# A two-block hybrid network on one core: the squares behind a norm are added up by VectorE, and one set of modulation columns is read later

## The reference

```python
mod = silu(c) @ ada_w + ada_b                  # 6 x 1024 columns per hybrid layer
sh_m, sc_m, gt_m, sh_f, sc_f, gt_f = split(mod, 6)
h = rms_norm(x, norm_mix) * (1 + sc_m) + sh_m
x = x + gt_m * (mixers(h @ w_in) @ w_out)      # attention, sparse attention, gated delta rule
h = rms_norm(x, norm_ffn) * (1 + sc_f) + sh_f
gate, up = split(h @ w_gate_up, 2)
x = x + gt_f * ((silu(gate) * up) @ w_down)    # two such layers, then a norm

x = x + attention(rmsnorm(x) @ w_in) @ w_o     # two layers of the second kind
x = x + (conv_gated(rmsnorm(x) @ w_up)) @ w_down
```

## Time and profile before

| | us |
|---|---|
| median of 3 runs (lowest, highest) | 1687.49 (1687.18, 1693.62) |
| the profiled execution, its own time | 1688.19 |
| its span in the profile | 1686.4 |
| PE busy in the span | 1531.1 |
| DVE busy | 1017.7 |
| ACT busy | 811.2 |
| POOL busy | 237.8 |

### The profile page before, as it was taken

How to read it: one execution, slowest core, us unless ns; L and a number is a source line. 1 busy time by engine, 2 the same in 40 slices (tenths; PEclk the granted TensorE clock), 3 DMA queues, 4 the chain that set the end, 5 groups by cost and what they waited for, 6 DMA issues and landing times.

```text
span 1686.4 us, 29656 instructions
## 1 busy us (share of the span) xinstructions
PE 1531.1 (91%) x12458; PEld 1454.6 (86%) x12458; DVE 1017.7 (60%) x1294; ACT 811.2 (48%) x1296; POOL 237.8 (14%) x96
## 2 busy tenths in 40 slices
PE   6989988899989999889999998489999999899997
PEld 3987778899989978789998897378999898799997
DVE  2775457867657645585545433957784545477843
ACT  3754354343347444444434343355664455466642
POOL 0002218534500022350000001210000001000000
PEclk8999999999999999999999898799999999999999
DMA  9435844645544365445347444013543633335442
GB/s 388 173 144 214 291 182 167 249 157 195 193 179 177 117 242 193 150 151 196 141 169 254 164 164 150 1 58 143 199 162 145 219 134 116 134 127 189 168 152 79
DMA packets 30336, 287.85 MB, mean 171 GB/s; under 512 B 2903, under 2 KB 11383, under 8 KB 11800
## 3 DMA queue, kind: packets, MB, share of 16 engines
q1 hardware_dynamic: 29032, 269.51, 43.3%
q0 software_dynamic: 1152, 16.78, 2.6%
q10 hardware_dynamic: 48, 0.05, 0.0%
HBM read 285.23 MB, written 7.39 MB: 174 GB/s over the span
## 4 chain that ended last, share of the span: by engine, by line
PE 77%; DVE 9%; ACT 5%; DMA 3%; issue 3%; POOL 3%; SPq 0%; DVEq 0%; ACTq 0%; POOLq 0%
PE bank L634 22%; PE bank L636 21%; PE bank L635 21%; PE bank L712 2%; DMA ring<-w_out 2%; DVE w_lo L1789 2%; ACT w_hi L1323 1%; PE bank L958 1%; DVE h L2255 1%; PE bank L792 1%; POOL arena L2352 1%; PE bank L736 1%; DMA arena<-ada 1%; POOL arena L2350 1%; PE bank L779 1%
## 5 line engine op out<-in xcount | busy, mean ns | idle before, releaser
L634 PE MATMUL bank<-hi_T,w_hi 128*128 128x256 f32 x2248 | 652.1, 290 | 38.9 <-DVE h_lo L1772 16.4
L636 PE MATMUL bank<-hi_T,w_lo 128*128 128x256 f32 x2248 | 646.5, 288 | 0.0
L1789 DVE TENSOR_TENSOR w_lo<-ring,w_hi 128x2048 fp32r<-128x2048 f32 (+2 forms) x224 | 519.2, 2327 | 199.8 <-ACT w_hi L1323 198.4
L635 PE MATMUL bank<-h_lo,w_hi 128*128 128x256 f32 x2056 | 592.4, 288 | 0.0
L1323 ACT ACTIVATE w_hi<-ring 128x2048 fp32r<-128x2048 f32 (+2 forms) x226 | 392.0, 1735 | 282.6 <-PE bank L636 271.7
L634 PEld LDWEIGHTS bank<-hi_T,w_hi 128*128 128x128 f32 x2248 | 442.4, 197 | 44.3 <-issue 27.8
L636 PEld LDWEIGHTS bank<-hi_T,w_lo 128*128 128x128 f32 x2248 | 441.8, 197 | 0.0
L635 PEld LDWEIGHTS bank<-h_lo,w_hi 128*128 128x128 f32 x2056 | 405.7, 197 | 0.2
L634 PE MATMUL bank<-act_hi,w_hi 128*128 128x256 f32 x704 | 201.1, 286 | 10.6 <-DVE act_lo L1808 8.9
L635 PE MATMUL bank<-act_lo,w_hi 128*128 128x256 f32 x704 | 200.3, 285 | 0.0
L636 PE MATMUL bank<-act_hi,w_lo 128*128 128x256 f32 x704 | 200.3, 285 | 0.0
(11 more groups left out here) (239 smaller groups left out, 1912.2 us busy)
## 6 DMA issues: line engine op xcount, KB each, us to landing
ring<-w_gu SPq DMA_DIRECT2D x22, 2048.0 KB, 7.7
ring<-w_dn SPq DMA_DIRECT2D x32, 1408.0 KB, 6.0
ring<-w_up SPq DMA_DIRECT2D x22, 2048.0 KB, 7.7
ring<-ada SPq DMA_DIRECT2D x16, 2048.0 KB, 8.9
ring<-w_mix SPq DMA_DIRECT2D x11, 2048.0 KB, 7.6
arena<-ada POOLq DMA_DIRECT2D x8, 2048.0 KB, 8.8
ring<-even_in SPq DMA_DIRECT2D x8, 2048.0 KB, 7.7
ring<-odd_in SPq DMA_DIRECT2D x6, 2048.0 KB, 7.7
```

The source lines that it names most:

```text
L634: nc.tensor.matmul(out, wh, xh, start=start, stop=False)
L635: nc.tensor.matmul(out, wh, xl, start=False, stop=False)
L636: return nc.tensor.matmul(out, wl, xh, start=False, stop=stop)
L1789: V.tensor_tensor(w_lo[:, n % SLOTS, at], ring[:, n % SLOTS, at], w_hi[:, u % AHEAD, 0:size].bitcast(F32), ALU.subtract).then_inc(w_lo_rea ...
```

## The change

In the eight norms behind a product, ACT still squares tiles 0 to 5 in pairs, but tiles 6 and 7 one by one. DVE adds the squares: after residual tile 4 it adds squared tiles 2, 3 onto 0, 1; after residual tile 6 it adds 4, 5 onto 0, 1 and then 1 onto 0. PE sums three tiles (0, 6, 7) and not eight. Apart from that, chunk 10 (22) of the modulation is no longer read by PE ahead of `up`: the loop of three turns is split into one turn and two, and the columns are made between them. Norms 0 and 5 stay as they were.

```diff
+    added = [n for n in range(len(norm_input)) if norm_input[n]]
+    sq_before = [sum(5 if norm_input[i] else 4 for i in range(n)) for n in range(len(norm_input))]
...
             def norm_sums(n):
                 for k in range(KT):
-                    if k % 2 == 0:
-                        pe.wait_ge(sq_ready, 4 * n + k // 2 + 1)
+                    if n in added:
+                        if 0 < k < KT - 2:
+                            continue
+                        if k == 0:
+                            pe.wait_ge(sq_added, added.index(n) + 1)
+                        else:
+                            pe.wait_ge(sq_ready, sq_before[n] + k - 2)
+                    elif k % 2 == 0:
+                        pe.wait_ge(sq_ready, sq_before[n] + k // 2 + 1)
                     last = nc.tensor.matmul(bank[:, 7, 0:S], const("ones"), h[:, k, :],
...
                 turns = 11 // SLOTS
                 pe.wait_ge(gemm_freed, t0)
-                with pe.Fori(0, turns) as i:
-                    for j in range(SLOTS):
-                        one(j, i * (2 * SLOTS) + u0 + 2 * j + 1, i * (4 * SLOTS) + t0 + 4 * j - 3)
+                def turn(first, end):
+                    with pe.Fori(first, end) as i:
+                        for j in range(SLOTS):
+                            one(j, i * (2 * SLOTS) + u0 + 2 * j + 1, i * (4 * SLOTS) + t0 + 4 * j - 3)
+
+                if m_next:
+                    turn(0, 1)
+                    modulations(m_next - 1, m_next)
+                    turn(1, turns)
+                else:
+                    turn(0, turns)
...
                 norm_sums(n + 1)
-                pe.wait_ge(std_ready, n + 2)
-                modulations(m + 6, m + 7)
                 up(f"gu{l}", norm_end[n + 1] - KT, m + 7)
...
+                        if j == 3:
+                            for k in (KT - 2, KT - 1):
+                                act.wait_ge(gemm_freed, ph["t0"] + k + 1)
+                                nc.scalar.activation(h[:, k, :], x[:, k, :], ACT.Square).then_inc(sq_ready, 1)
+                            continue
                         act.wait_ge(gemm_freed, ph["t0"] + 2 * j + 2)
...
                     for u in used:
                         if u < ph["u1"] - 1:
                             low(u + AHEAD)
+                    if k in (4, 6):
+                        dve.wait_ge(sq_ready, sq_before[norm_input.index(name)] + k // 2)
+                        ch(V.tensor_tensor(h[:, 0:2, :], h[:, 0:2, :], h[:, k - 2:k, :], ALU.add))
+                    if k == 6:
+                        V.tensor_tensor(h[:, 0, :], h[:, 0, :], h[:, 1, :], ALU.add).then_inc(sq_added, 1)
```

More of the change, by code:

```diff
@@ L331, in hybrid_then_mixture @@
         sq_ready = sem("sq_ready")
+        sq_added = sem("sq_added")
         ssq_ready = sem("ssq_ready")
```

## The result

The changed kernel took 1697.72 us in the median of 10 runs (1692.49 to 1702.81), the kernel before 1687.99 us in the same comparison (10 runs, 1676.16 to 1693.62). The ratio is 1.0054, 95% interval 1.0033 to 1.0076: slower by 9 us, where I had forecast 26. Measured a second time it was 1696.16 us, ratio 1.0088 (1.0057 to 1.0119). The profiled execution took 1692.59 us, its span is 1690.8 us, 4.4 us more than before. It is one of the two fastest of the ten, so the profile shows less than half of the 9.7 us between the medians; what happened in the slower executions, no trace shows.

The account below looks back on a forecast made before the run. The prediction took PE, with 77% of the chain of waits, to bound the kernel: matmuls with holes. Its terms, 1688.2 - 5.9 - 0.1 + 18 + 17 + 1.6 - 5 = 1713.8, gave 1714 us, range 1682 to 1724.

Parts of the forecast that it names:

- The plain norms, -5.9: In dn0, dn1, o0, down0 and down1, the root no longer waits for PE and the last square is shorter: minus 5.9 us.
- o1, -0.1: In the norm after o1, VectorE's sums delay residual tile 7 and take back the gain of 1.2 us: minus 0.1 us.
- The sums in out0 and out1 wait for POOL: Behind out0, VectorE's sums wait for POOL's instructions, so the root starts 8 us late; the same steps behind out1.
- The next product falls into the normalise steps: Behind out0 and out1, POOL's next product begins at 278.6 and 729.9 us, before VectorE's last low part.
- Each remaining step alternates with one POOL instruction: Behind out0 and out1, remaining VectorE steps let in POOL instructions of 6.9, 4.4, 2.2, 1.1 us; terms plus 18, plus 17.
- none hits: Rival: POOL's products miss the normalise steps behind out0 and out1, leaving about 5 us each; 1692 us, chance 0.12.
- The columns moved, +1.6: Four column matmuls between two full tiles of `up` take about 0.8 us of PE, twice: plus 1.6 us.
- The stalls in `up`, -5: In `up`, PE's loads wait 10.2 us for VectorE's gate product; two of four weighings remain, so half goes: minus 5 us.
- Cheap sums: Rival: POOL does not hold the sums behind out0 and out1; 1684 us, chance 0.21, of which 0.09 at or below 1679.
- The table load: Rival: in plain norms the table load moves behind the wait, so they do not shorten; plus 6 us, no chance given.
- The clock behind the longer holes: Rival: PE's clock falls for longer behind holes of 7 us, up to 3 us for each of two norms; no chance given.
- the case that I held most likely: Both POOL products, behind out0 and out1, fall into the normalise steps; 1714 us, own range 1704 to 1724, chance 0.55.

Follow-up runs that it names:

- plain_norms_only: The changed kernel with the old eight-tile sums behind out0 and out1, new sums in the six other norms; 1679.1 us, ratio 0.9930.
- pieces_old_sums: The changed kernel with the old sums in all norms, GpSimd's product in four pieces and its first sum in two; 1673.42 us, ratio 0.9920.
- columns_only: The kernel before with only the columns moved and the loop split, no new sums; 1680.68 us, ratio 0.9929; repeated, 1683.99 us, ratio 0.9984.
- gpsimd_at_root: The changed kernel with GpSimd's product of chunk 10 (22) held until the root of the norm behind out is made; 1689.68 us.

## Why the prediction was wrong

Its own steps, in its own order:

- **The plain norms, -5.9: right, mechanism and size.** The idle time before the root went from 0.93 to 1.07 us to 0.01 us in all five; the roots come 6.1 us earlier in all, the 48th matmuls (behind down1, the root) 5.5 us. That is read between the marks; in the medians a gain of this size did not show (`plain_norms_only`, `pieces_old_sums`).
- **o1, -0.1: right.** The root is 0.07 us earlier, the 48th matmul 0.05 us later.
- **The sums in out0 and out1 wait for POOL: right.** I had put the end of sum 1 0.55 us behind POOL's product, and residual tile 7 at 270.5; it came at 269.4, and POOL had started 0.8 us earlier. In out1 the lengths are the same to 0.01 us.
- **The next product falls into the normalise steps: right.** Forecast 278.6 and 729.9, measured 278.29 and 730.04.
- **"Each remaining step alternates with one POOL instruction": wrong, and this is the step that failed.** It was taken from the waits in the earlier trace rows, in which POOL was already at work when VectorE asked. The reverse stands there once, POOL's product coming 0.36 us into the low part at 250.10 and reading 8.80 us for 7.01, but with no second such instruction right behind that one. Nothing shows POOL coming to a VectorE in full run, and I used the same rule for that. In all four arrivals traced in the changed kernel POOL stayed out, not a step was held, and 18 and 17 us became 6.4 and 7.5. The 21 us between are all but the whole error of the profiled execution (forecast +25.6 against +4.4 in the span). In the medians the error is 16 us; their executions are some 5 us slower than the profiled one, and no trace shows why. Had I bounded the step from both sides, as I should have, the lower end (the row of steps undisturbed, the first low part 5.4 us late; measured 275.96 for 270.21, 5.75) was already worked out in the text. Even the rival "none hits" kept the wrong rule: it wanted the product to come later, not to stay out. The sums of this step were also a little off by their own terms (280.8 and the four instructions let in make 295.4, not 295.0; in out1 three steps can let in only three instructions), which changes less than 1 us.
- **The columns moved, +1.6: wrong sign.** About -5 us in the profiles, all of it in layer 0; the medians leave it open. I had priced eight matmul records and nothing that they set free. Ahead of `up` the first matmul comes 0.6 us earlier, at 11.6 us for 12.2, but the 48th at 19.3 and 18.8 us in `columns_only` and at 18.8 twice in its repeat, 19.25 before, as more matmuls behind the hole run at the lower clock (14 to 20 for 12). Between out0's 48th matmul and the end of dn0, PE's holes of over 1 us add up to 10.2 and 8.1 us against 14.2 before, and 31 and 39 matmuls stand at the lower clock's pace against 59.
- **The stalls in `up`, -5: right in size (10.2 to 4.9 us), by luck, as the cause was wrong.** In `columns_only` and its repeat these waits are 4.5 and 2.8 us too, and there the weighing of chunk 11 has not moved into the norm; with the sums alone they are 7.9. So most of it comes with the column move, and the sum of the two terms, -3.4, stands against a measured -4.5 (both stretches from the 48th matmul to the end of the down product).
- **The rivals.** "Cheap sums" is refuted (7.12 us). The table load did not move. "None hits" names nearly the time of the profiled execution, 1692 for 1692.6, by a road that it did not take: both products came when I said, so the near hit is luck. What I held against it was thin, too: the DMA waits that I quoted spread by 1 us, but the eight of the whole trace before go from 7.14 to 11.65 us. The clock behind the longer holes cost little: of the first 48 matmuls 16 and 25 ran at the lower clock's pace, 12 and 12 before, and from the first to the 48th it took 0.3 and 1.1 us more, where the rival had up to 3. The median lies in my range of 1682 to 1724 only because the range took in the rivals; the case that I held most likely had 1704 to 1724.

What is not settled: how much the column move and the new sums of the plain norms are worth to better than 7 us in the medians, and why the column move shortens the stalls.

## What to carry to other kernels

Where VectorE and GpSimd both have two inputs in SBUF, look for who was first: rows in which VectorE waits for GpSimd say nothing of what happens when GpSimd arrives second, and that case needs its own bound. Long GpSimd operations beside a serial chain are best cut into pieces of the length that the chain can stand; here pieces of 1.9 us took the changed kernel from 1698 to 1672 us, 26 us, and the change that they repaired had cost 9. When a gain goes at a place where a helper's product is awaited, follow the helper to its last use: in both kernels that held GpSimd back, part of the delay came out as waits or a hole further on.

## What the runs showed of the hardware

- A VectorE add of 512 elements with both inputs in SBUF takes 0.68 us alone and 7.12 us beside a GpSimd product that has begun (7.01 us long alone); it ends 0.56 us behind the end of that instruction. The Trainium skill, "SBUF — State Buffer", section "SBUF: two separate sides", says that whichever starts first has the shared ports for the whole instruction and the other fully blocks; for a VectorE instruction that comes second the trace agrees.
- By that rule a waiting GpSimd instruction should be served when VectorE's present step ends. In 12 of 16 arrivals it was not: in all 12 it ended 6.88 us behind the low part of 128x2048 that follows the 16 steps (283.40 and 290.28 for an arrival at 278.29), so it had waited out the steps and that low part, though the steps ended 0.40 us apart. In the other four, the early ones, it got in at the next step. Once VectorE had been held, the two alternated instruction by instruction, in every place seen (5.63, 4.72, 2.56, 1.48 us in gpsimd_at_root).
- POOL's spans include its waiting: the same product reads 7.01 us alone and up to 12.71 us when it is kept out.
